# Retention outputs in the PSUM banks of their scores, operand splits on GpSimd, and moved TensorE fillings

## The reference, cut to what matters

```python
def first_block(x, ...):                       # one layer, T = 1024 tokens, width 1024
    hn = rms_norm(h, norm_mix_pre); p_rw, p_ret, g_rw, g_ret = split(hn @ w_in)
    y_rw  = rwkv7_mixer(p_rw, ...)             # 8 heads of 64; group norm, bonus, then times g
    y_ret = retention_mixer(p_ret, positions)  # 8 heads, chunks of 128 tokens, silu(g) * group_norm(o)
    merged = sigmoid(g_rw) * (y_rw @ w_branch_rw) + sigmoid(g_ret) * (y_ret @ w_branch_ret)
    h = h + rms_norm(merged @ w_out, norm_mix_post)
    f = conv_ffn(rms_norm(h, norm_ffn_pre), w_up, conv_w, conv_b, w_down)
    return h + rms_norm(f, norm_ffn_post)

def retention step of a chunk:                 # per head, R is the 64 x 128 state
    s = (q k^T) * decay_mask; inner = s v; cross = (q * q_decay) R
    R = R * chunk_decay + (k * k_decay)^T v;   out = inner + cross

def second_block(x, ...):                      # pooling mixer and sliding-window attention
    y = concat(pool_out, attn_out) @ w_out;    return x + rms_norm(y, norm_post)
```

## Time and profile before

| what | us |
|---|---|
| median of 3 runs | 2414.36 |
| lowest, highest | 2413.3, 2414.92 |
| the profiled execution, its own time | 2412.11 |
| its span, first to last instruction | 2410.3 |
| PE busy in it | 2356.0 |

### The profile page before, as it was taken

How to read it: one execution, slowest core, us unless ns; L and a number is a source line. 1 busy time by engine, 2 the same in 40 slices (tenths; PEclk the granted TensorE clock), 3 DMA queues, 4 the chain that set the end, 5 groups by cost and what they waited for, 6 DMA issues and landing times.

```text
span 2410.3 us, 33719 instructions
## 1 busy us (share of the span) xinstructions
PE 2356.0 (98%) x12944; PEld 1918.1 (80%) x12944; DVE 1377.7 (57%) x1562; ACT 658.0 (27%) x1064; POOL 790.9 (33%) x420
## 2 busy tenths in 40 slices
PE   7999999999999999999999999999999999999997
PEld 6888888888887887887787788888878787777775
DVE  7755465446545644766558744544541387657766
ACT  4312121121113112443242211111122445114441
POOL 2311231222113114113465333333334445422154
PEclk9999999999999999999999999999999999999998
DMA  3211211121111115645434111111124333211023
GB/s 143 68 53 53 71 55 51 53 71 53 56 59 62 62 45 180 210 145 202 155 130 150 53 47 49 44 52 44 46 76 141 120 120 95 64 63 44 27 79 113
DMA packets 61904, 205.22 MB, mean 85 GB/s; under 512 B 6240, under 2 KB 10464, under 8 KB 61152
## 3 DMA queue, kind: packets, MB, share of 16 engines
q1 hardware_dynamic: 40560, 138.76, 18.5%
q10 hardware_dynamic: 21232, 64.80, 7.3%
HBM read 167.36 MB, written 36.18 MB: 84 GB/s over the span
## 4 chain that ended last, share of the span: by engine, by line
PE 90%; DVE 6%; ACT 2%; DVEq 1%; issue 1%; DMA 0%; POOL 0%; ACTq 0%; POOLq 0%
PE psg L477 10%; PE psg L482 10%; PE psg L481 10%; PE psg L609 7%; PE psg L614 6%; PE psg L616 6%; PE psa L709 1%; PE psg L1205 1%; PE psg L1198 1%; PE psg L571 1%; PE psg L574 1%; PE psg L1203 1%; PE psg L575 1%; PE psb L696 1%; PE psg L1249 1%; PE psg L1243 1%
## 5 line engine op out<-in xcount | busy, mean ns | idle before, releaser
L402 POOL CAST whi<-wraw 128x1024 fp32r<-128x1024 f32 (+1 forms) x176 | 192.2, 1092 | 1397.2 <-PE psg L609 516.8
L404 POOL TENSOR_TENSOR wlo<-wraw,whi 128x1024 fp32r<-128x1024 f32 (+1 forms) x176 | 460.7, 2618 | 25.4 <-issue 0.2
L477 PE MATMUL psg<-xhi,whi 128*128 128x512 f32 x1008 | 401.9, 399 | 3.0 <-issue 1.4
L482 PE MATMUL psg<-xhi,wlo 128*128 128x512 f32 x1008 | 398.3, 395 | 0.0
L481 PE MATMUL psg<-xlo,whi 128*128 128x512 f32 x1008 | 396.0, 393 | 0.0
L609 PE MATMUL psg<-xhi,whi 128*128 128x512 f32 x640 | 261.0, 408 | 0.0
L616 PE MATMUL psg<-xhi,wlo 128*128 128x512 f32 x640 | 259.7, 406 | 0.0
L614 PE MATMUL psg<-xlo,whi 128*128 128x512 f32 x640 | 257.0, 402 | 0.0
L477 PEld LDWEIGHTS psg<-xhi,whi 128*128 128x128 f32 x1008 | 189.2, 188 | 49.1 <-issue 4.5
L482 PEld LDWEIGHTS psg<-xhi,wlo 128*128 128x128 f32 x1008 | 189.2, 188 | 47.7
L481 PEld LDWEIGHTS psg<-xlo,whi 128*128 128x128 f32 x1008 | 189.2, 188 | 46.5 <-issue 0.7
(11 more groups left out here) (612 smaller groups left out, 4812.8 us busy)
## 6 DMA issues: line engine op xcount, KB each, us to landing
wraw<-w SPq DMA_DIRECT2D x224, 512.0 KB, 3.5
later_scratch<-stage ACTq DMA_DIRECT2D x40, 512.0 KB, 2.6
xres<-xt ACTq DMA_DIRECT2D x4, 1024.0 KB, 10.7
RV<-later_scratch SPq DMA_DIRECT2D x4, 1024.0 KB, 11.4
RG<-later_scratch SPq DMA_DIRECT2D x4, 1024.0 KB, 6.3
later_scratch<-rstage ACTq DMA_DIRECT2D x8, 512.0 KB, 2.6
mgr<-later_scratch ACTq DMA_DIRECT2D x8, 512.0 KB, 3.6
mgt<-later_scratch ACTq DMA_DIRECT2D x8, 512.0 KB, 4.6
```

The costliest lines, as they stand in the source:

```text
L402: pool.tensor_copy(whi[:, u, 0:width], wraw[:, u, 0:width])
L404: pool.tensor_tensor(wlo[:, u, 0:width], wraw[:, u, 0:width], whi[:, u, 0:width].bitcast(F32), ALU.subtract).then_inc(w_ready, 1)
L477: mm = pe.matmul(ps[:, cols], whi[:, slot, w_cols], rhs_hi(k, cols), start=(k == 0), stop=False)
L482: mm = pe.matmul(ps[:, cols], wlo[:, slot, w_cols], rhs_hi(k, cols), start=False, stop=(k == kts - 1))
```

## The change

Ten edits, in program order:

1. RWKV pair, DVE: the two `normed_half(LATER - 1)` go in front of the multiplication that raises `gn_nrm`. ACT's `store_later(LATER - 1)` goes in front of its wait for `gn_nrm`, and the store of `YB` goes to the top of the next turn of the loop, so the last pair's `YB` isn't stored. A store of zeros in the first turn takes its place, and DVE zeroes `YB` once at the program's start.
2. Retention: POOL makes all four `xhi` of the branch's operand, and `xlo` 0 and 1; DVE makes `xlo` 2 and 3; ACT makes none. POOL does this ahead of the split of the branch's first weight block.
3. The first `w_used` of the branch moves from its first matmul to the first of `ret_values(0, 0)`.
4. Head 0's outputs go to `psa`, the banks of its scores; values of pairs 1 to 3 go to `psa`, norm sums and spreads to `psb`; `r_states` is waited for after head 0's outputs, ahead of the cross terms.
5. In pairs 1 to 3 the portions are 12 ahead of the keys, none between key-value products and outputs (before: 8 after the keys and 4 there), and the keys move from the end of pair p to pair p + 1, behind that portion and behind the wait for `yret_done`.
6. `merge_feature(1, ..)` uses `psa` in place of `psb`.
7. Output product: half of block 1 (12 matmuls) is done ahead of the last 3 of block 0; `w_used` of block 1 is raised at its second half.
8. FFN up and second layer: the second spread of the norm factor is done ahead of the last 6 matmuls of its block, not behind them.
9. `mix_block(0)`: the norm sums go ahead of the last 6 matmuls, not of the last 3.
10. Attention: the last portion is 38 matmuls, not 24.

```diff
+            pool.wait_ge(g_full, T_BRW)
+            pool.wait_ge(sem("yrw_in"), 16 * (PAIRS - 1))
+            for j in range(PAIRS):
+                if j == PAIRS - 1:
+                    pool.wait_ge(sem("yrw_done"), PAIRS + 1)
+                pool.tensor_copy(xhi[:, j, :], yrw[j][:, :])
+            pool.drain()
+            for j in range(PAIRS // 2):
+                pool.tensor_tensor(xlo[:, j, :], yrw[j][:, :], xhi[:, j, :].bitcast(F32), ALU.subtract
+                                   ).then_inc(sem("y_pool"), 1)
             split_blocks(B_BRW, B_MRG, PAIRS * P)
...
-                        pe.wait_ge(sem("op_split"), SPLIT_BEFORE["yrw"] + PAIRS)
+                        pe.wait_ge(sem("y_pool"), PAIRS // 2)
+                        pe.wait_ge(sem("op_split"), PAIRS // 2)
...
-            out_t = [psb_t, psc_t]
+            out_t = [psa_t, psc_t]
...
                 if p:
-                    fill_branch(8)
+                    fill_branch(12)
                     pe.wait_ge(sem("yret_done"), 2 * p)
+                    ret_keys(p)
...
-                fill_branch(4 if p else 0)
                 for n, h in enumerate((1, 0)):
                     pe.wait_ge(sem("rs_ready"), 2 * p + n + 1)
-                    if h == 0:
-                        pe.wait_ge(sem("r_states"), p + 1)
                     for c in range(NB):
                         pe.matmul(out_t[h][:, c, :], RVT[:, h, c, :], RP[h][:, c, :], start=(c % 4 == 0), stop=False)
+                pe.wait_ge(sem("r_states"), p + 1)
                 pe.wait_ge(sem("rqd"), p + 1)
...
-            for k in range(KT):
+            for k in range(KT - 1):
                 pe.wait_ge(sem("op_split"), SPLIT_BEFORE["merged"] + k + 1)
                 out_block(0, (k,))
-            for n in range(1, KT + 1):
+            out_ready(1)
+            out_block(1, range(LATE), begins=KT)
+            pe.wait_ge(sem("op_split"), SPLIT_BEFORE["merged"] + KT)
+            out_block(0, (KT - 1,))
+            out_block(1, range(LATE, KT), begins=LATE)
+            for n in range(2, KT + 1):
...
-            up_block(AGAIN + 2, range(KT // 2, KT)).then_inc(g_full, 1)
+            up_block(AGAIN + 2, range(KT // 2, KT - 2))
             pe.wait_ge(sem("pre_added"), 2 * KT + 1)
             half_spread(1, prstd[:, HALF:T])
+            up_block(AGAIN + 2, range(KT - 2, KT)).then_inc(g_full, 1)
...
-                        fill(24 if n == 4 * PAIRS - 1 else 10)
+                        fill(38 if n == 4 * PAIRS - 1 else 10)
...
+                for half in range(2):
+                    normed_half(LATER - 1, half)
                 tt(YB[:, :], YB[:, :], flat(psa), MUL).then_inc(sem("gn_nrm"), 1)
...
                 tt(YB[:, :], YB[:, :], G[:, :], MUL).then_inc(sem("yrw_done"), 1)
-                for half in range(2):
-                    normed_half(LATER - 1, half)
...
-                    for j in range(PAIRS):
-                        operand_low("yrw", j, yrw[j][:, :], j)
+                    v.wait_ge(sem("y_pool"), PAIRS // 2)
+                    for j in range(PAIRS // 2, PAIRS):
+                        tt(xlo[:, j, :], yrw[j][:, :], xhi[:, j, :].bitcast(F32), SUB).then_inc(sem("op_split"), 1)
...
-            s.wait_ge(sem("yrw_in"), 16 * (PAIRS - 1))
-            for j in range(PAIRS):
-                operand_high(yrw[j][:, :], j)
```

More of the change, by code:

```diff
@@ L358, in _ @@
             load_gates(0)
[L359 removed]
+            sp.wait_ge(sem("yrw_done"), PAIRS + 1)
             sp.wait_ge(sem("rv_tr"), 2)
@@ L817, in branch_products @@
                                            start=(k == 0), stop=False)
-                            if half == 0 and k == 0:
+                            if j and half == 0 and k == 0:
                                 mm.then_inc(w_used, 1)
@@ L853, in ret_values @@
                     mm = pe.matmul(dst[:, c, :], RV[:, h, c * P:c * P + P], RC[:, :], start=True, stop=True)
+                    if p == 0 and h == 0 and c == 0:
+                        mm.then_inc(w_used, 1)
                 mm.then_inc(sem("rv_tr"), 1)
@@ L939, in merge_feature @@
                     w_cols = slice(k * P, (k + 1) * P)
-                    dst = psb[:, half, :] if u else psg[0][:, cols]
+                    dst = psa[:, half, :] if u else psg[0][:, cols]
                     mm = pe.matmul(dst, whi[:, u, w_cols], xhi[:, k, cols], start=(k == MERGE_K[0]), stop=False)
@@ L1360, in _ @@
             v.memset(SC[:, :, :], 0.0)
+            v.memset(YB[:, :], 0.0).then_inc(sem("yrw_done"), 1)
             v.wait_ge(sem("pos_in"), 32)
```

63 lines of the change are left out of this document (31 added, 32 removed).

## The result

The changed kernel takes 2398.21 us (median of four runs, 2397.27 to 2399.33) against 2414.31 for the kernel before on the same chip: ratio 0.9933, 95% interval 0.9917 to 0.9949. It is faster by 16.1 us; the prediction was 2401.2, with a range of 2396.5 to 2406.5. The profiled execution took 2399.33 us, with a span of 2397.5.

The account below looks back on a forecast made before the run. PE bounds the kernel, busy 2356.0 of 2410.3 us, so only idle time and slow clock can change. 5.7 + 2.6 - 0.5 + 2.3 + 3.1 = 13.2 us off 2414.4 gives 2401.2, range 2396.5 to 2406.5.

Parts of the forecast that it names:

- First pair: Retention's first pair, edits 1 to 4: waits and slow clock go; gain 5.7 us, bounds 3.9 and 7.3.
- rivals 4 and 5: Ahead of first filling, POOL's chain eats whole gain, 2412.7 us, chance 0.04; or longer still, 2418 us, chance 0.02.
- only the order of the pieces changes: Ahead of the first filling: if DVE's subtractions get in before POOL's work, the sum of 5.7 us stands.
- Pairs 1 to 3: Edits 4 and 5: waits for `r_states` and the values' copy go; gain 2.6 us, bounds 0 and 2.7.
- The three norm spreads: Edits 8 and 9: waits for `frs`, `drstd` and `hexp` covered by matmuls; gain 2.3 us, bounds 1.3 to 2.5.
- keys wait for `yret_done`: Pairs 1 to 3: new wait on DVE's two multiplications, 2.6 us in all, covered by twelve matmuls by 0.1 or 0.2.
- pairs 1 to 3 gain nothing: Rival for the retention's later pairs: `yret_done`, keys' copy or decayed scores come late; 2403.8 us, chance 0.12.
- Output product: Edits 6 and 7: new wait of 1.5 us for block 2; loss 0.5 us, bounds gain 1.0, loss 1.4.
- Last step: Last attention step, edit 10: idle 2.82 us covered and clock kept; gain 3.1 us, bounds 1.6 and 3.2.
- At nothing: Zeroing `YB`, store of zeros and later store: no cost; 1.3 us a pair if their cover were gone.
- Rival 1: Clock falls in new waits (keys, first filling, block 2), 1.7 us a drop; up to 2404.6 us, chance 0.15.
- Rival 2: No new wait at first filling or output product's block 2, POOL being sooner; 2398.1 us, chance 0.12.

Follow-up runs that it names:

- more groups: Changed kernel with six more switches between groups of matmuls in the retention (pairs 0 to 2), the work the same: 2414.31 us, ratio to before 1.0002.
- the later store: Changed kernel with the store of `YB` moved on ScalarE from the top of the turn to behind the square of `KK`: 2396.85 us.

## Why the prediction was right, and where it was off

**First pair: 5.7 predicted, 6.03 measured.** The step held. The second values start behind the first, the clock stays, the keys wait 1.26 (predicted 1.2) and the first filling 1.78 (1.6). Edit 1 alone brings 5.28 of it. Counted from the spread, POOL's L443 ended at 13.45 and its first L405 at 15.42, for 13.7 and 15.6 in the prediction, so rivals 4 and 5, POOL's chain eating the gain, are out. The words that "only the order of the pieces changes" if DVE gets in first are borne out in three profiles below, and there the filling came 0.45 sooner. What I had not seen is what edit 2 guards: not the 0.75 us of waiting so much as the 1.5 of slow clock that stood behind the longer wait.

**Pairs 1 to 3: 2.6 predicted, 3.88 measured.** The mechanism is right and the term mis-sized: it was the sum of the waits shown. From the spread to the filling behind the outputs, pair 1 has 15.24 us before and 14.09 after. Taken apart by PE's starts: spread to what follows 1.28 to 0.80 (a wait of 0.24 shown, 0.48 gone); fillings 2.05 + 1.04 to 2.88; keys 0.84 to 1.00; first outputs 2.43 to 1.89 (0.49 shown, 0.54 gone); second outputs 1.96 to 1.88. So 0.2 more than the shown waits, and 0.2 for one portion fewer. A row's idle time starts at the end of the work ahead, while unhindered PE starts the next group before that end: in the timeline above L865 starts at 958.13 and the group ahead of it ends at 958.30. A removed wait gives back that overlap too. The three norm spreads say the same: 0.9, 0.5 and 0.9 were shown, 1.13, 0.73 and 1.16 came back. I had 2.3 there and it was 3.0. That accounts for 0.7 there and, with the portion fewer, for the 1.3 in the pairs. These 2.0 and the first pair's 0.3 are set against 0.45 at the end and small misses elsewhere, which makes the 1.8 between 13.2 and 15.0. For the cost of one more portion there is one experiment beside these rows: with edit 5 undone the three pairs were 0.5 us longer than their three waits. Its portions of 8 and 4 took 2.04 and 1.03 between PE's starts, against 2.88 for the 12: 0.2 again. What else changed in that kernel partly cancels, so this is read from rows and not from the total.

**That edit 4 needs edit 5** stood in the prediction as "keys wait for `yret_done`", and in my expectation for edit 5 undone I forgot it. The run put 7.9 us on it. The rival "pairs 1 to 3 gain nothing" was nearer than its 0.12 looks: the cover is 0.08 us wide.

**Output product: 0.5 lost predicted, 0.40 measured,** with the wait that was named (1.21 for 1.5). **Last step: 3.1 predicted, 2.92 measured,** with its wait of 1.22 for 1.3.

**At nothing.** YB's memset and the later stores: the RWKV stage of the kernel before took 939.49 us in its one profile, and 940.5 on average in the thirteen with any of the edits (939.48 to 941.40). A loss of up to 1 us is neither shown nor excluded. "In the first product of a pair" does not hold for the first pair's store of zeros: ACT's first mix stands behind it, and PE waits 0.3 to 0.8 for that mix in the eleven profiles with that order.

**Rival 1** (the clock falls in a new wait) did not come at the three waits it named. It came at a fourth place: the last four transposes, behind two waits of 1.5 and 1.2 that both kernels have, run at .50 in nine of thirteen profiles with any of the edits and at 1.00 in the kernel before. It costs 0.45. **Rival 2** asked for the waits to be absent; they were there.

**The range.** Its low end does not follow from its words. Rival 2 gives 2398.1, and the upper bounds of the other parts take off another 0.1, 0.2 and 0.1, which is 2397.7 and not 2396.5. The medians of 2398.21 and 2398.00 lie above both. The predicted 2401.2 was 3.0 too high: 1.8 of it is the sum, and the rest lies in the time ahead of the first spread and in the distance of the profiled executions from their medians, for which the prediction had no term.

## What to carry to other kernels

A removed wait is worth what its row shows plus some 0.2 us of overlap, and another 1.5 to 3 when the clock would have fallen behind it (1.5 with edit 2 undone, 1.7 before, 3.0 with more groups). Before two edits are judged apart, look at which banks and buffers tie them; here the new banks without the moved keys cost 2.6 us in each of three pairs. Before a few tenths are put down to an edit, see whether the same place moves by as much without it. And small units of filler are not interchangeable: ask which of them ends a block, and what the engine that empties the block has queued behind it.

## What was new about the hardware

**The clock and the length of a wait.** Behind PE's waits of 2.54, 2.56, 2.61, 2.82, 2.91 and 4.56 the granted clock fell to .50, and behind all between 1.0 and 1.6 it stayed at 1.00, but for the two at the very end. In between both were seen: behind the same wait for the first filling it stayed in four profiles with 1.78 and fell in one with 1.79. And three waits of 2.61 to 2.62 in the kernel with edit 5 undone left it at 1.00, where two of 2.61 in the kernel with more groups did not. The window that holds the first of the three:

```profile
994.00:997.00 3.00, 2.40 (x15) 2.13 (x16) 1.68 (x2) 1.25 (x2) 0.76 (x2) 1.00 1.04 378
```

The length of the wait alone does not decide. What does is left open; a term for the clock in a sum of this kind is a chance, not a number. The runs of one kernel may differ in it too: with more groups they lie 8.4 us apart, with edit 1 alone 5.0, and the changed kernel's nine within 2.1.

**GpSimd and VectorE on two SBUF operands.** In the changed kernel a subtraction of 1.22 us on DVE that starts with one of 1.27 on POOL takes 2.32: it ends about 1.1 after POOL's end, as if it had begun there. POOL ran at full speed meanwhile, and its own two subtractions of operand tiles took 4.70 beside DVE's work with a PSUM input, about twice the 2.37 and 2.39 of the earlier trace rows. The Trainium skill, "SBUF — State Buffer", section "Who interferes with whom", says that one of the two blocks fully and that the first to issue has the port. The rows agree that one stands still: either DVE takes 2.32 and POOL 1.27, or DVE takes 1.22 and POOL 2.35 or 2.36. Which of them it is was not settled by the program. In eight profiles POOL went first, in three (edit 5 undone, edit 7 undone, the later store) DVE did, and the first filling stood at 17.74 or 17.75 for 18.19. The profile puts POOL's start 0.02 or 0.03 us ahead in the eight and 0.01 or 0.02 in the three, so at this distance its starts don't tell who had the port, and the order of issue is neither borne out nor refuted.
